# Routing, x updates and the end of the experts in a two-block transformer kernel: reordered steps on one Trainium2 core

## What is computed

```python
x = x + g1[:, None, :] * y                       # y: output projection of the attention
h = modulate(rmsnorm(x, norm_ffn[i]), sh2, sc2)  # h * (1 + sc2) + sh2
y = hier_moe(h, w_rg, b_rg, w_re, b_re, w_gate, w_up, w_down)
x = x + g2[:, None, :] * y

# hier_moe: g_idx = argmax of 4 group logits; e_sel = the 4 expert logits of that group
top_v, top_i = lax.top_k(e_sel, EXPERT_TOP_K)    # ties go to the first
top_w = jax.nn.softmax(top_v, axis=-1)
hid = silu(t @ w_gate[e]) * (t @ w_up[e]) * gates[:, e]
y = sum over e of hid @ w_down[e]
```

## Time and profile before

| | us |
|---|---|
| median of 3 runs | 1765.79 (1765.11 to 1766.05) |
| the profiled execution | 1767.12 |
| its span, first to last instruction | 1765.3 |
| TensorE busy | 1719.4 (97%), granted clock 0.994 |
| VectorE, ScalarE, GpSimd busy | 1189.5, 896.0, 251.4 |

### The profile page before, as it was taken

One profiled execution on the slowest core, in us unless ns is written; L12 is line 12 of the kernel. 1 busy time (PEld: TensorE's weight loads), 2 busy tenths in 40 slices (PEclk: granted clock), 3 DMA queues, 4 the chain that ended last, 5 costly groups with the idle time before them and its releaser, 6 DMA issues.

```text
span 1765.3 us, 25730 instructions
## 1 busy us (share of the span) xinstructions
PE 1719.4 (97%) x8552; PEld 1356.7 (77%) x8552; DVE 1189.5 (67%) x1816; ACT 896.0 (51%) x1322; POOL 251.4 (14%) x232
## 2 busy tenths in 40 slices
PE   6999989999999999999999999999999999999999
PEld 5777767788888877667788888887775888888887
DVE  6777775798989983555677777225797577777422
ACT  4466652688888743664444444214665444444310
POOL 0000000234343300001100000001895100000000
PEclk8999999999999999999999999999999999999999
DMA  9833214999999932111223333331662323333331
GB/s 394 310 96 96 72 53 139 338 386 388 384 386 377 340 113 79 60 61 56 88 95 95 95 95 97 119 96 59 162 154 71 96 88 101 98 95 95 120 95 59
DMA packets 79860, 273.66 MB, mean 155 GB/s; under 512 B 11244, under 2 KB 11500, under 8 KB 78512
## 3 DMA queue, kind: packets, MB, share of 16 engines
q1 hardware_dynamic: 75040, 264.61, 43.8%
q0 software_dynamic: 4464, 7.60, 1.1%
q10 hardware_dynamic: 288, 0.54, 0.1%
HBM read 256.02 MB, written 16.80 MB: 155 GB/s over the span
## 4 chain that ended last, share of the span: by engine, by line
PE 88%; DVE 5%; ACT 3%; issue 2%; DMA 2%; POOL 0%; SPq 0%; DVEq 0%; ACTq 0%; POOLq 0%
PE ps L1161 20%; PE ps L1163 20%; PE ps L1162 20%; PE ps L1433 3%; PE ps L1432 3%; PE ps L1431 3%; PE ps L1223 2%; PE ps L1244 2%; PE ps L1457 1%; PE ps L1455 1%; PE ps L1456 1%; PE ps L1182 1%; PE ps L1183 1%; PE ps L1184 1%; PE ps L1814 1%
## 5 line engine op out<-in xcount | busy, mean ns | idle before, releaser
L1161 PE MATMUL ps<-h_hi,w_hi 128*128 128x512 f32 x1120 | 445.7, 398 | 2.0 <-DVEq L2469 1.2
L1163 PE MATMUL ps<-h_hi,w_lo 128*128 128x512 f32 x1120 | 437.2, 390 | 0.0
L1162 PE MATMUL ps<-h_lo,w_hi 128*128 128x512 f32 x1120 | 437.0, 390 | 0.0
L142 DVE TENSOR_TENSOR w_lo<-raw,w_hi 128x1024 fp32r<-128x1024 f32 x212 | 276.2, 1304 | 170.9 <-ACT w_hi L137 170.6
L137 ACT ACTIVATE w_hi<-raw 128x1024 fp32r<-128x1024 f32 x212 | 222.1, 1049 | 176.5 <-PE ps L1163 156.4
L1161 PEld LDWEIGHTS ps<-h_hi,w_hi 128*128 128x128 f32 x1120 | 210.6, 188 | 71.5 <-issue 28.6
L1163 PEld LDWEIGHTS ps<-h_hi,w_lo 128*128 128x128 f32 x1120 | 210.6, 188 | 45.0
L1162 PEld LDWEIGHTS ps<-h_lo,w_hi 128*128 128x128 f32 x1120 | 210.9, 188 | 42.0 <-issue 0.5
L182 DVE TENSOR_TENSOR w_lo<-ring,w_hi 128x1024 fp32r<-128x1024 f32 x128 | 149.6, 1220 | 23.8 <-ACT w_hi L178 23.8
L1024 ACT ACTIVATE tmp<-ps,param 128x512 f32<-128x512 f32 x88 | 68.7, 780 | 185.6 <-DVE ps L2435 185.6
L2443 DVE SCALAR_TENSOR_TENSOR tmp<-ps,param,tmp 128x511 f32<-128x511 f32 (+1 forms) x176 | 131.8, 749 | 17.6 <-DVE tmp L2443 3.1
(11 more groups left out here) (398 smaller groups left out, 2809.1 us busy)
## 6 DMA issues: line engine op xcount, KB each, us to landing
ring<-in_w_m SPq DMA_DIRECT2D x192, 512.0 KB, 6.9
raw<-in_w_b SPq DMA_DIRECT2D x180, 512.0 KB, 3.5
raw<-in_w_a SPq DMA_DIRECT2D x32, 512.0 KB, 4.2
ada_late<-in_ada_b SPq DMA_DIRECT2D x32, 512.0 KB, 4.6
ada<-in_ada_a SPq DMA_DIRECT2D x8, 1024.0 KB, 20.9
shifted<-glu SPq DMA_DIRECT2D x24, 260.0 KB, 4.8
y_dram<-o SPq DMA_DIRECT2D x8, 512.0 KB, 9.3
y_tok<-y_dram SPq DMA_DIRECT2D x8, 512.0 KB, 8.1
```

What stands on the lines that cost most here:

```text
L142: dve.tensor_tensor(self.lo[:, s, :], self.raw[:, s, :], self.hi[:, s, :].bitcast(F32), ALU.subtract).then_inc(self.lo_done, 1)
L1161: pe.matmul(dst, hi, a_hi, start=first, stop=False, skip_group_check=True)
L1162: pe.matmul(dst, hi, a_lo, start=False, stop=False, skip_group_check=True)
L1163: return pe.matmul(dst, lo, a_hi, start=False, stop=last, skip_group_check=True)
```

## The change

Parts of it: (1) VectorE's x updates of chunks 0 and 1 stand ahead of the adaLN columns, later ones behind fewer of them. (2) SP writes and reads the shift row ahead of the last twelve adaLN loads, and waits for the first x update before. (3) `add_shift` is made of products of 32 rows: four rows hold high and low parts of root and shift, marked by `row_kind`. (4) Turnings of the third token block stand ahead of the last x update. (5) The choice is made in all groups at once and masked by the group afterwards, in two alternating chains of steps. (6) Rounds and `first_of` stand ahead of the gates and the other tables; the slot sums stand between the halves of the gather, and the fetch of expert 1's tokens is turned behind the first chunk of expert 0's up projection. (7) The four token stores stand ahead of ring loads 8 to 11. (8) In the last expert the counter and the tables of a next round stand after split 3 of 12, and the low half of its hidden earlier; the slot sums behind the loop go. (9) VectorE adds all four blocks of y. Cut to its core:

```diff
@@ SP
-            for n in range(n, 4 * KC):
-                load_late(n)
             sp.wait_ge(late_done, 2 * KC)
+            sp.wait_ge(x_new, 1)
             sp.dma_start(s_dram..., mod[:, 3 * KC:4 * KC]).then_inc(shift_in, 16)
             sp.wait_ge(shift_in, 16)
             sp.dma_start(shift_read[:], ...).then_inc(shift_in, 16)
+            for n in range(n, 4 * KC):
+                load_late(n)
...
-            store_tokens(0)
-            store_tokens(1)
-            for c in (8, 9):
-                sm.load(sp, 0, 0, c)
-            store_tokens(2)
-            store_tokens(3)
-            for c in (10, 11):
+            for t in range(NT):
+                store_tokens(t)
+            for c in range(8, RING):
                 sm.load(sp, 0, 0, c)
@@ PE
+            pe.wait_ge(x_new, KC - 1)
+            for k in range(KC // 2):
+                turn_scaled(k, 2)
             pe.wait_ge(x_new, KC)
...
             def add_shift(t):
-                pe.wait_ge(std_split, t + 1)
+                rows = slice(32 * t, 32 * (t + 1))
                 for b in range(2):
-                    last = pe.matmul(ps[...], std_of[:, t], shift_rows[:, b * T:(b + 1) * T], ...)
+                    last = pe.matmul(ps[...], std_parts[rows, 1], e_lo[rows, b * NT:(b + 1) * NT], ...)
...
             add_shift(1)
+            add_shift(2)
+            pe.wait_ge(rstd_done, 2)
+            unread(1, SSQ)
...
             add_shift(3)
+            unread(2, SSQ)
...
-            slots_of(2)
...
-                pe.wait_ge(onehot_done, r * 3 + 3)
-                pe.wait_ge(e_lo_done, n + 1)
                 for b in range(2):
...
+                    if b == 0:
+                        slots_of(r * 3 + 3)
@@ DVE
             link(dve.tensor_tensor(lg[:], lg[:], over(router_c, 1, TN), ALU.add))
+            step_a = step(dve.tensor_tensor(by_group(key), all_lg, over(tops, 3, G4), ALU.is_equal))
+            dve.wait_ge(route, step_g)
+            step_g = step(dve.tensor_tensor(group_key, group_lg, over(group_top, 2, T4), ALU.is_equal))
+            dve.wait_ge(route, step_a)
...
+            dve.wait_ge(router_mm, 2)
+            step_a = step(dve.tensor_reduce(out=rounds_f[:, 0:1], ...))
+            step_g = step(dve.scalar_tensor_tensor(out=pos_first, ...))
...
+            dve.tensor_copy(rounds[:], rounds_f[:, 3:4]).then_inc(rounds_done, 1)
...
+            first_wanted()
             dve.wait_ge(route_exp, 2)
...
+                    if last and c == 10:
+                        next_round(r)
+                    if last and c == 17:
+                        hidden_lo(n, e_hi[:, 0:FEC], e_lo[:, 0:FEC])
...
-                if c == 8:
+                if c == 9:
                         expert_tokens_lo(r * NE + 1)
...
-            dve.wait_ge(y_loaded[NT - 1], 16 + 32)
-            dve.wait_ge(y_added, NT - 1)
-            dve.tensor_tensor(y_tok[:, 0, NT - 1], ...)
+            for t in range(NT):
+                dve.wait_ge(y_loaded[t], 16 + 32)
+                dve.tensor_tensor(y_tok[:, 0, t], y_tok[:, 0, t], y_tok[:, 1, t], ALU.add).then_inc(y_added, 1)
@@ ACT
+                act.wait_ge(rows_known, ROW_STEPS)
+                act.activation(e_hi[:], by_chunks, ACT.Copy).then_inc(shift_done, 1)
+                act.activation(shift_rows[:]..., by_chunks, ACT.Copy, scale=shift_lo_row).then_inc(shift_done, 1)
...
-            for t in range(NT):
-                act.activation(std_of[:, t], std, ACT.Copy, scale=C("pick", t * P, 1)).then_inc(std_split, 1)
+            act.activation(std_parts[:, 0], std, ACT.Copy).then_inc(std_hi_done, 1)
+            act.activation(rstd, std, ACT.Copy, scale=std_lo_row).then_inc(std_hi_done, 1)
...
+                    if c == 18 and last:
+                        hidden_hi(n, e_hi[:, 0:FEC])
```

More of the change, by code:

```diff
@@ new lines, in by_four, with each @@
+            def by_four(values):
+                return values.rearrange("p t (g e) -> p (t g) e", g=NG)
+            def each(values):
+                return over(values.rearrange("p t g -> p (t g)"), 2, [P, NT * NG, 4])
+            group, group_top, group_key, group_max = r44[:, 3], r4[:, 0], r44[:, 2], r4[:, 1]
+            tops, tops2, key_max = r44[:, 4], r44[:, 6], r44[:, 5]
+            key, choice1, choice2 = r16[:, 0], r16[:, 1], r16[:, 2]
+            rest = pos_of[:, 0]
+            pri_all = over(C("pri"), 1, [P, NT * NG, 4])
@@ new lines, in _ @@
+            all_lg, group_lg = by_group(lg[:, :, NG:]), lg[:, :, 0:NG]
+            dve.tensor_reduce(out=tops, in_=all_lg, axis=AX.X, op=ALU.max).then_inc(route, 1)
+            step_a = steps[0] + 1
+            steps[0] = step_a
+            step_g = step(dve.tensor_reduce(out=group_top, in_=group_lg, axis=AX.X, op=ALU.max))
+            dve.wait_ge(route, step_a)
+            step_a = step(dve.tensor_tensor(by_group(key), all_lg, over(tops, 3, G4), ALU.is_equal))
+            dve.wait_ge(route, step_g)
@@ new lines, in _ @@
+            step_g = step(dve.tensor_tensor(group_key, group_lg, over(group_top, 2, T4), ALU.is_equal))
+            dve.wait_ge(route, step_a)
+            step_a = step(dve.tensor_tensor(by_four(key), by_four(key), pri_all, ALU.mult))
+            dve.wait_ge(route, step_g)
+            step_g = step(dve.tensor_tensor(group_key, group_key, pri, ALU.mult))
+            dve.wait_ge(route, step_a)
+            step_a = step(dve.tensor_reduce(out=key_max, in_=by_group(key), axis=AX.X, op=ALU.max))
@@ new lines, in _ @@
+            dve.wait_ge(route, step_g)
+            step_g = step(dve.tensor_reduce(out=group_max, in_=group_key, axis=AX.X, op=ALU.max))
+            dve.wait_ge(route, step_a)
+            step_a = step(dve.tensor_tensor(by_four(choice1), by_four(key), each(key_max), ALU.is_equal))
+            dve.wait_ge(route, step_g)
+            step_g = step(dve.tensor_tensor(group, group_key, over(group_max, 2, T4), ALU.is_equal))
+            dve.wait_ge(route, step_a)
+            step_a = step(dve.scalar_tensor_tensor(out=by_group(rest), in0=by_group(choice1), scalar=-BIG, in1=all_lg, op0=ALU.mult,
+                                                   op1=ALU.add))
@@ new lines, in _ @@
+            dve.tensor_tensor(r44[:, 0], group_lg, over(group_top, 2, T4), ALU.subtract).then_inc(route_sel, 1)
+            dve.wait_ge(route, step_a)
+            step_a = step(dve.tensor_reduce(out=tops2, in_=by_group(rest), axis=AX.X, op=ALU.max))
+            step_g = step(dve.tensor_tensor(by_group(choice1), by_group(choice1), over(group, 3, G4), ALU.mult))
+            dve.wait_ge(route, step_a)
+            step_a = step(dve.tensor_tensor(by_four(key), by_four(rest), each(tops2), ALU.is_equal))
@@ new lines, in _ @@
+            step_g = step(dve.tensor_tensor(r44[:, 7], tops2, tops, ALU.subtract))
+            dve.wait_ge(route, step_a)
+            step_a = step(dve.tensor_tensor(by_four(key), by_four(key), pri_all, ALU.mult))
+            dve.wait_ge(route, step_g)
+            step_g = step(dve.tensor_tensor(r44[:, 7], r44[:, 7], group, ALU.mult))
+            dve.wait_ge(route, step_a)
+            step_a = step(dve.tensor_reduce(out=key_max, in_=by_group(key), axis=AX.X, op=ALU.max))
+            dve.wait_ge(route, step_g)
@@ new lines, in _ @@
+            dve.tensor_reduce(out=r4[:, 8], in_=r44[:, 7], axis=AX.X, op=ALU.add).then_inc(route_sel, 1)
+            dve.wait_ge(route, step_a)
+            link(dve.tensor_tensor(by_four(choice2), by_four(key), each(key_max), ALU.is_equal))
+            link(dve.tensor_tensor(by_group(choice2), by_group(choice2), over(group, 3, G4), ALU.mult))
+            dve.tensor_tensor(r16[:, 0], r16[:, 1], r16[:, 2], ALU.add).then_inc(route_sel, 1)
+            step(dve.tensor_tensor(fields(0), chosen_twice, for_both(numbers[:].rearrange("p f n t -> p f (n t)")), ALU.mult))
```

240 lines of the change are left out of this document (127 added, 113 removed).

## The result

The changed kernel takes **1756.76 us** (median of 5 runs, 1755.25 to 1757.95), the kernel before 1766.05 in the same rounds: 0.9948 of it, 95% interval 0.9938 to 0.9959. The forecast was 1755.0, with a range of 1751.5 to 1759.5. The medians differ by 9.3; the profiled executions, 1767.12 and 1756.76, by 10.4; the forecast sum was 10.9.

A forecast was written before the change was run, and what follows sets the result against it. The prediction took TensorE's own time, idle time and clock to bound the kernel. Its terms, -3.8 - 4.5 - 2.6 = -10.9, took the median of 1765.79 to 1754.9, say 1755.0 us, range 1751.5 to 1759.5.

The forecast's parts named there:

- early x updates: Projections: TensorE's idle 2.04 us before the third chunk's sums and 1.8 of half clock go, -3.8 us.
- gather, after x(7): Routing: the first gather starts 12.25 us after the last x update instead of 16.8, 4.5 sooner.
- wait for the fetch: First expert: TensorE's wait for the second expert's fetched tokens costs from nothing to 0.3 us.
- from x(7) to the last expert: Routing and experts: -4.6 us since the last x update, less 0.1 for the fetch, kept through the experts.
- stall before e_hid is turned: Last expert: the next round's counter and tables on VectorE leave TensorE idle for 1.9 us.
- turning of y sooner, at full clock: Behind the last expert: y turned at 622.4 instead of 623.45, -1.05; 32 turnings at full clock, -1.5.
- covered as well: Projections: SP's shift row ahead of the twelve adaLN loads costs nothing, with 2 us in hand.
- risk to the gain diagonals: Projections: late adaLN loads, behind the row's write, make TensorE wait near 281; 1771 us, chance 0.02.
- The last lands at about 18 at the latest: Routing: the last token store lands about 18 us after the last x update, before the slot rows are known at 18.2.
- rivals with a fallen clock: Last expert: the clock falls at TensorE's 1.9 us stall, costing 1.8; 1756.8 us, chance 0.13.
- chains that don't overlap: Routing: the choice takes 5.7 us instead of 3.6, +2.1; 1757.1 us, chance 0.10.
- experts' stage bound by DMA: Experts: DMA at 383 GB/s sets the pace and the 4.5 is lost in weight waits; 1759.5 us, chance 0.07.

The follow-up runs named there:

- e1: Changed kernel with VectorE's x updates back behind the adaLN columns and the shift row behind the twelve adaLN loads: 1760.58 us.
- e2: Changed kernel with only SP's order undone, the shift row behind the twelve adaLN loads and x updates still early: 1765.18 us.
- e9: Changed kernel with the shift row behind the adaLN loads, its copies behind the square of x(6) and its product behind x(7): 1758.97 us.
- e3: Changed kernel with the choice as one chain, each step waiting for the one before: 1761.81 us.
- e7: Changed kernel with the rounds and their cast computed behind all slot tables, the first table still early: 1761.47 us.
- e5: Changed kernel with ring loads 6 and 7 issued behind the four token stores instead of ahead of them: 1754.99 us.
- e11: Changed kernel with expert 1's tokens turned one part later, behind half of expert 0's second product instead of a quarter: 1757.94 us.
- e4: Changed kernel with the next round's counter and tables left out: 1754.80 us.
- e10: Changed kernel with the next round's tables ahead of the last expert's first part instead of behind its third: 1754.73 us.
- e6: Changed kernel without the unread products ahead of the gather and the experts' loop: 1754.72 us.
- e8: Changed kernel with three of the four sums of y back on GpSimd: 1760.23 us.
- e12: Changed kernel with both the next round's tables ahead of the last expert and expert 1's tokens turned one part later: 1753.56 us.

## Why the prediction was right, step by step

| step | forecast | measured |
|---|---|---|
| early x updates | -3.8 | -3.4 in the traces (307.44 against 310.88); undone in e1, 3.1 to 3.4 by the traces |
| shift passes, all four blocks | 1.8 or less | 1.34 (six products from 310.55 and two from 316.57, 0.67 each time to the next start) |
| route products, after x(7) | 7.3 | 6.93 |
| gather, after x(7) | 12.25 | 11.62 |
| first expert's products | 20.9 | 19.57 |
| wait for the fetch | 0 to 0.3 | **1.42** |
| from x(7) to the last expert | -4.5 | -4.21: 283.30 against 287.51 |
| stall before e_hid is turned | 1.9 | 1.66 |
| turning of y sooner, at full clock | -1.05 and -1.5 | -1.42 and -1.35 |
| sum | -10.9 | -10.4 |

*Early x updates.* Right in size, and the wait is the cause. That half clock follows the wait held for the kernel before and not for e1, where 2.88 us left the clock up. I had named the row's write and the twelve loads as "covered as well". They are, in the order that the change chose; e2 and e9 show that the cover is that order, and that moving the columns makes the loads, and all behind them, 14 us later (the row is written at 295.3 in e2, at 281.4 in e1). I had seen the queue only as a risk to the gain diagonals.

*Choice and rounds.* The two chains overlap (e3), the gather hangs on the cast (e7), and both came out a little shorter than I had them: 3.23 for the choice instead of 3.6, and 7.95 for gather and slot sums instead of 8.65, since I had added durations whose ends overlap the next start.

*The fetch* is the one term that was mis-sized, 1.42 for a forecast 0 to 0.3. "The last lands at about 18 at the latest" was wrong: the last store was issued at 318.5 and landed 8.5 us later, at 327.0, which is 19.6 on that scale (GpSimd waited for it until 327.91), and TensorE came 1.3 sooner than I had it. The two errors hide each other: what TensorE gained ahead of the fetch it spent waiting for it. e5 adds that an earlier issue alone doesn't help; asking later does in the trace of e11.

*The end.* The stall is VectorE's tables (e4, e10), and the clock did not fall behind its 1.66 us. The rivals with a fallen clock, with chains that don't overlap and with an experts' stage bound by DMA did not come: A keeps what the start wins, with 244 of 244 us busy at 385 GB/s.

*The clock.* That it stayed up is in part luck. I had gone by the length of the wait, between 1.52 and 2.04, and the runs show that the length does not decide: the clock stayed up behind 2.88 us (e1) and 3.05 (e9), and fell behind 1.50 (e6), 2.54 (e3), 3.81 (e8), 4.16 (e7) and 5.26 (e2). In e12 it fell in the routing behind the same waits of 0.20 and 0.66 that left it up in the changed kernel.

Open: why some executions lose the clock at 289 us with TensorE busy, and others, with the same instructions, don't. No run here tells. Parts (3), (4) and (7) of the change were not undone alone, so what each of them adds to the 4.21 is not shown.

## What to carry to other kernels

When work moves behind other work on an engine, follow the buffers that it frees: here twelve loads in SyncE's queue hung on it, and a row behind them fed copies that stood ahead of the critical squares. Look for a later step's home where the engine already waits (the tables into VectorE's 1.60 us), and ask for a transfer later before trying to send it sooner (1.34 in the trace of e11, nothing in that of e5). Compare stage times within traces, not medians, where an effect is under 2 us, and set aside the stretches where the clock alone differs.

## What was not expected of the hardware

- The granted clock was 0.50 from 286 to 292 us in three executions (e3, e4, e11) in which TensorE was busy for all of that time.
- It stayed full behind an idle 2.88 us (e1) and 3.05 (e9) and fell behind 1.50 (e6) and 2.04 (the kernel before).
- ScalarE's two copies of the row in another order of its elements take 2.05 to 2.2 us for 128x1024, where a plain copy of as much takes 1.05 (L137); e2 and the changed kernel.
- A wait for the step before costs VectorE 0.08 to 0.12 us a step on operations of 16 to 64 elements (e3).
- A fetch sent 1.4 us sooner, with the DMA at 400 GB/s, landed at the same time, though the store in front of it landed 3.8 us sooner after its issue (e5).
- A GpSimd sum of two SBUF tiles (3.39 us) cost VectorE's three splits beside it 2.1 us (e8).
